# Moving residual additions, lambda's arithmetic, two weight splits and one product group in a two-layer decoder trunk on one NeuronCore

## The reference

```
proj = rmsnorm(x, g_mix[1]) @ w_in_b          # 768 differential queries, 256 memory queries
q    = rope(proj[..., :768])
lam  = exp(sum(lq1*lk1)) - exp(sum(lq2*lk2)) + lambda_init
p    = softmax(causal(q k^T / 8))             # 12 heads of 64, in pairs
a    = p[:, :, 0] - lam * p[:, :, 1]          # 6 pairs
o    = rmsnorm(a v, g_subln) * (1 - lambda_init)
m    = memory attention, 4 heads
x    = x + concat(o, m) @ w_out[1]
x    = x + top-2-of-8 expert SwiGLU(rmsnorm(x)), expert width 3584
out  = rmsnorm(x, g_final)
```

## Time and profile before

| | |
|---|---|
| median of 3 runs | 1523.36 us (1522.26 to 1524.27) |
| the profiled execution | 1524.27 us, span 1522.5 us |
| PE busy | 1460.5 us (96%) |
| DVE busy | 1147.5 us (75%) |
| ACT busy | 961.2 us (63%) |
| chain that ended last | PE 90%, DVE 5%, ACT 3% of the span |
| experts | from 542 to 1514 us of the span |

### The profile page before, as it was taken

The page is one execution under the profiler, slowest core; times in us unless marked ns, Lnnn a source line. Parts: engine busy times, 40 slices in busy tenths (PEclk is TensorE's granted clock), DMA queues, the critical chain, the costliest instruction groups (busy, mean ns, idle before and its releaser), DMA issues.

```text
span 1522.5 us, 19748 instructions
## 1 busy us (share of the span) xinstructions
PE 1460.5 (96%) x7414; PEld 1231.5 (81%) x7414; DVE 1147.5 (75%) x944; ACT 961.2 (63%) x883; POOL 24.4 (2%) x40
## 2 busy tenths in 40 slices
PE   7998899999898899999999999999999999999996
PEld 7975699999687678888888888888888888888885
DVE  4554444454667489889879879989988988987985
ACT  5652334434476387687777778677768678767773
POOL 1000020000000010000000000000000000000000
PEclk9995899999899899999999999999999999999999
DMA  9750275555532289999989999998998998998991
GB/s 298 256 186 28 84 273 170 170 194 181 175 112 83 98 315 388 396 326 394 396 321 373 395 376 343 393 379 328 396 390 310 393 396 323 387 396 322 391 396 40
DMA packets 204356, 440.42 MB, mean 289 GB/s; under 512 B 9232, under 2 KB 43184, under 8 KB 204304
## 3 DMA queue, kind: packets, MB, share of 16 engines
q1 hardware_dynamic: 201008, 428.37, 77.0%
q0 software_dynamic: 3296, 11.33, 2.1%
HBM read 430.76 MB, written 8.91 MB: 289 GB/s over the span
## 4 chain that ended last, share of the span: by engine, by line
PE 90%; DVE 5%; ACT 3%; issue 1%; DMA 0%; DVEq 0%; SPq 0%; ACTq 0%
PE ps L1422 28%; PE ps L1424 27%; PE ps L1423 27%; PE ps L1914 2%; DVE w_lo L881 1%; PE ps L1567 1%; ACT w_hi L496 1%; DVE H L912 1%; PE ps L1540 1%; PE ps L1448 1%; PE ps L1620 0%; PE ps L1884 0%; DMA raw<-in_w_mem_kv_dram 0%; ACT H L521 0%; PE ps L1885 0%
## 5 line engine op out<-in xcount | busy, mean ns | idle before, releaser
L1344 DVE TENSOR_TENSOR e_wlo<-raw,e_whi 128x2048 fp32r<-128x2048 f32 x336 | 751.1, 2285 | 89.7 <-ACT e_whi L815 89.7
L815 ACT ACTIVATE e_whi<-raw 128x2048 fp32r<-128x2048 f32 x336 | 621.0, 1915 | 39.7 <-PE ps L1424 37.0
L1422 PE MATMUL ps<-e_whi,act_hi 128*128 128x512 f32 x1344 | 529.0, 394 | 2.0 <-DVE act_lo L1300 1.5
L1424 PE MATMUL ps<-e_wlo,act_hi 128*128 128x512 f32 x1344 | 523.8, 390 | 0.0
L1423 PE MATMUL ps<-e_whi,act_lo 128*128 128x512 f32 x1344 | 523.2, 389 | 0.0
L1422 PEld LDWEIGHTS ps<-e_whi,act_hi 128*128 128x128 f32 x1344 | 252.4, 188 | 54.5 <-issue 3.0
L1424 PEld LDWEIGHTS ps<-e_wlo,act_hi 128*128 128x128 f32 x1344 | 252.3, 188 | 53.4
L1423 PEld LDWEIGHTS ps<-e_whi,act_lo 128*128 128x128 f32 x1344 | 252.5, 188 | 50.7
L881 DVE TENSOR_TENSOR w_lo<-raw,w_hi 128x2048 fp32r<-128x2048 f32 (+2 forms) x68 | 148.5, 2198 | 141.7 <-ACT w_hi L496 141.3
L496 ACT ACTIVATE w_hi<-raw 128x2048 fp32r<-128x2048 f32 (+2 forms) x68 | 124.1, 1839 | 66.8 <-PE ps L1424 59.1
L820 ACT ACTIVATE act_hi<-ps 128x512 fp32r<-128x512 f32 x56 | 33.6, 599 | 183.1 <-PE ps L1914 183.0
(11 more groups left out here) (243 smaller groups left out, 1091.9 us busy)
## 6 DMA issues: line engine op xcount, KB each, us to landing
raw<-in_w_exp_gate_dram SPq DMA_DIRECT2D x112, 1024.0 KB, 7.9
raw<-in_w_exp_up_dram SPq DMA_DIRECT2D x112, 1024.0 KB, 8.6
raw<-in_w_exp_down_dram SPq DMA_DIRECT2D x112, 1024.0 KB, 9.4
raw<-in_w_dense_gate_dram SPq DMA_DIRECT2D x11, 1024.0 KB, 5.4
raw<-in_w_dense_up_dram SPq DMA_DIRECT2D x11, 1024.0 KB, 5.4
raw<-in_w_dense_down_dram SPq DMA_DIRECT2D x11, 1024.0 KB, 5.8
raw<-in_w_out_dram SPq DMA_DIRECT2D x8, 1024.0 KB, 5.0
raw<-in_w_in_a_dram SPq DMA_DIRECT2D x7, 1024.0 KB, 9.7
```

The source lines that it names most:

```text
L815: nc.scalar.activation(e_whi[:, (s - NPRE) % E_SPLIT, :], raw[:, s % RAW, :], ACT.Copy)\
L1344: nc.vector.tensor_tensor(e_wlo[:, r, :], raw[:, s % RAW, :], e_whi[:, r, :].bitcast(F32), ALU.subtract).then_inc(lo_ready, 1)
L1422: nc.tensor.matmul(dst, l_hi, r_hi, start=start, stop=False)
L1424: return nc.tensor.matmul(dst, l_hi, r_lo, start=False, stop=stop)
```

## The change

It does five things. (1) The residual additions of both tiles stand before the normalisation of either, in all places where they were interleaved (`sums` is gone from `norm`). (2) VectorE's three lambda instructions, with their wait for `lam_a`, stand right behind the rotation of the second query tile. (3) VectorE writes slot o+2's remainder at i = D0 + 4 in place of D0 + 6. (4) Slot o+3 is split by ScalarE and VectorE inside the loop at i = D0 + 9, and TensorE does `memory_out(1)` inside the loop at i = D0 + 8, before that. (5) `heads_turn(1)` stands behind the two `out_product(2, ...)` in place of before them.

```
 ACT        if i == D0 + 4:
                split_to(o + 3)
+           if i == D0 + 9:
+               split_to(o + 4)
 ...
            head_rms(1)
-           split_to(o + 4)
            heads_high(1)

 DVE        def norm(signal, streams, new=True):       # sums=None is gone
                n = norms[0]
+               dve.wait_ge(gain_in, 16 * (n + 1))
                for t in range(TT):
-                   if sums is not None:
-                       sums(t)
-                   if t == 0:
-                       dve.wait_ge(gain_in, 16 * (n + 1))
 ...
+           dve.wait_ge(tile0_done, 2)
+           for half in range(2):
+               residual(0, half, 4 + half)
+           dve.wait_ge(slot_used, b)
+           for half in range(2):
+               residual(1, half, 6 + half)
+           norm(h_ready, 3)
-           norm(h_ready, 3, sums=dense_sums)
 ...
            rope(q_raw, 1, 20)
+           dve.wait_ge(lam_a, 1)
+           link(nc.vector.tensor_tensor(lamc[:, 4:5], lamc[:, 3:4], lamc[:, 2:3], ALU.subtract))
+           link(nc.vector.tensor_scalar(lamc[:, 5:6], lamc[:, 4:5], -LAMBDA_INIT, None, ALU.add))
+           link(nc.vector.tensor_scalar(gsub[:, :], gsub[:, :], 1.0 - LAMBDA_INIT, None, ALU.mult))
            split_to(k + 4)
            rope(k_raw, 2, 21)
            unit_max(NU0)
 ...        (the same four lines taken out behind unit_max(D0 + 1))
                if i == D0 + 4:
                    dve.wait_ge(mem_hi, 1)
                    nc.vector.tensor_tensor(act_lo[:, 6:8, :], ...).then_inc(mem_lo, 1)
-               if i == D0 + 6:
                    split_to(o + 3)
+               if i == D0 + 9:
+                   split_to(o + 4)
 ...
            head_norm(1)
-           split_to(o + 4)
            heads_low(1)

 PE             if i == D0 + 6:
                    pe.wait_ge(mem_lo, 1)
                    w_mem = take()
                    memory_out(0, w_mem)
+               if i == D0 + 8:
+                   memory_out(1, w_mem)
            heads_turn(0)
-           memory_out(1, w_mem)
            w0, w1 = take(), take()
            pe.wait_ge(heads_lo, 1)
            ...                                     # out_product(0), (1)
-           heads_turn(1)
            for t in range(TT):
                out_product(2, t, w1, 0)
+           heads_turn(1)
```

More of the change, by code:

```diff
@@ L899, in _, with norm @@
             norms = [0]
-            def norm(signal, streams, new=True, sums=None):
+            def norm(signal, streams, new=True):
                 n = norms[0]
+                dve.wait_ge(gain_in, 16 * (n + 1))
                 for t in range(TT):
[L905 to L908, removed]
                     if new:
@@ L919, in residual, with out_residual @@
                 nc.vector.tensor_tensor(xs, xs, ps[:, bank, :], ALU.add).then_inc(add_done, 1)
+            def out_residual(n, end):
+                dve.wait_ge(slot_used, end - 2)
+                for t in range(TT):
+                    residual(t, 0, 4 + t)
+                split_to(min(end + 2, NPRE))
+                dve.wait_ge(tile0_done, 2 * n + 1)
+                residual(0, 1, 6)
+                dve.wait_ge(slot_used, end)
+                residual(1, 1, 7)
             def unit_max(u):
@@ L1086, in _ @@
             split_to(first["dense"] + 1)
[L1087 to L1100, removed]
+            out_residual(0, first["dense"])
+            norm(h_ready, 2)
             turn()
@@ L1236, in _ @@
             head_norm(1)
-            split_to(o + 4)
             heads_low(1)
             split_to(NPRE)
-            def out_b_sums(t):
-                if t == 0:
-                    dve.wait_ge(tile0_done, 3)
-                else:
-                    dve.wait_ge(slot_used, o + 4)
-                for half in range(2):
-                    residual(t, half, ACC_BANK[t, half])
-            norm(h_ready, 4, sums=out_b_sums)
+            dve.wait_ge(tile0_done, 3)
+            for half in range(2):
+                residual(0, half, ACC_BANK[0, half])
+            dve.wait_ge(slot_used, o + 4)
+            for half in range(2):
+                residual(1, half, ACC_BANK[1, half])
+            norm(h_ready, 4)
             turn()
```

8 lines of the change are left out of this document (2 added, 6 removed).

## The result

The changed kernel takes **1537.22 us**, the median of four runs (1535.72 to 1537.95), beside 1523.82 (four runs, 1522.26 to 1524.3) for the kernel before: a ratio of 1.0091, 95% interval 1.0079 to 1.0103, or 13.9 us more. (The ratio is estimated over all runs of both kernels and is not the quotient of the two medians, which lie 13.4 apart.) The profiled execution took 1539.68 with a span of 1537.8, so from profile to profile the span grew by 15.3, where the sum of the terms was 15.1.

The account below looks back on a forecast made before the run. TensorE was taken as full in the experts and from 434 to 472 us, with engines waiting in turn from 472 to 494. Terms summed to +15.1 us on a median of 1523.36, giving 1538.5, range 1532.5 to 1544.0.

Parts of the forecast that it names:

- the clock holds: Rival: TensorE's clock stays up in all new gaps; +11.2 us in all, 1534.6; chance 0.20.
- A: After the first output projection: tile 1's addition fits ahead of tile 0's normalisation, next product earlier; -2.1 us.
- B: After the dense part: both additions fit before tile 0's root, transposes' copies come earlier; -2.5 us.
- N: Before the router: tile 0's normalisation already fits beside tile 1's products, exchange only moves a wait; 0 us.
- L: Before memory attention: VectorE's early lambda wait delays a key-weight slot, a maximum and unit 4's transposes; +5.5 us.
- C: Loop: slot o+2's early remainder waits for ScalarE, delaying unit 12's transposes 3.4, plus slow clock; +4.6 us.
- D: Loop: the second memory half's 12 products are hidden by nothing; +2.7 us.
- E: Loop: slot o+3's remainder waits for ScalarE and holds up the maximum of unit 18; +4.3 us.
- T: Tail: TensorE waits for both heads' remainders with nothing hiding them, partly at slow clock; +2.6 us.
- the second memory half runs at half clock too: Rival: the clock falls in each gap and through these loop products as well; +21.7 us, 1545; chance 0.10.
- Spare time: Rival: idle time in and before the loop absorbs the moved work; -6.1 us, 1517.3; chance 0.03.
- The parts don't overlap: Denies a rival: parts overlap, leaving one loop remainder's cost and half of lambda's; about +6 us, 1529.5; chance 0.07.

Follow-up runs that it names:

- The filled wait: Kernel before with slot o+2's remainder moved early and 16 unused 512-column products ahead of the waiting transposes: 1523.15 us, ratio 1.0019.
- The filled kernel: Kernel before with additions first, 6 memory products moved into the loop, and 18 or 19 unused transposes at each of three waits: 1508.92 us, ratio 0.9911.

## Why the prediction was right

The forecast was 1538.5, and 1537.22 came; of the rivals the nearest is 2.6 away (the clock holds, 1534.6). From the memory remainder to the heads' transposes the loop is 13.1 longer, where 9 to 14 were said. Step by step, each term as a difference of two steps' starts in the two traces:

| term | predicted | found | range stated |
|---|---|---|---|
| A additions, first output projection | -2.1 | -2.2 | -2.3 to -0.8 |
| B additions, dense | -2.5 | -2.3 | -2.7 to -1.2 |
| N additions, router | 0 | -0.2 | -0.3 to +1.3 |
| L lambda | +5.5 | +5.4 | 3.9 to 6.5 |
| C slot o+2's remainder | +4.6 | +6.3 | 3.4 to 5.9 |
| D memory half | +2.7 | +2.8 | 2.0 to 5.2 |
| E slot o+3 | +4.3 | +4.1 | 3.9 to 5.0 |
| T tail | +2.6 | +2.9 | 0.7 to 3.1 |

**A and B** came out as the in-order reasoning has it, and the additions alone show them again (-2.2 and -2.7). **D, E** are repeated by the two kernels that have them alone (+2.45, and 4.4 on top). **T**: two gaps of 2.11, "near 2 us twice"; the wait for the remainder took 3.65 from the heads' transposes (3.62 was said), the 36 products 10.41 (10.1), the last transposes' way 2.93 (2.9).

**L came out by another path than the one worked.** Its idle times are what was said (9.10 for "some 9", 3.52 for "near 4"), and the maximum is 5.8 late. But the prediction has the transposes wait for that maximum's chain ("follow the reciprocal", 5.1 late), and they don't. Before, the reciprocal was over at 442.36 and TensorE, busy without a break, reached the transposes only at 443.21; now it is over at 441.13 and they start at 441.60, again with no idle time ahead. What makes them late is TensorE itself: its slot's first product comes 3.87 later behind the scores of unit 4, and the 12 products at the lower clock add 1.49. That the two ways give 5.1 and 5.4 is chance; with the clock held, the chain would have been the later of the two, by some 1.2 (an estimate: 441.60 less 1.49, beside 441.13 and 0.15 to the start).

**C was mis-sized**, and lies outside its own bounds. Its idle part is what was said (the transposes +3.34 later relative to the memory remainder, "+3.4"). The clock part was taken as a half-way value of 1.2 and given at most 2.5; it measured 2.95: the 12 products behind the gap took 5.13 instead of 2.82 (+2.31), and the values ahead of them were slow as well (+0.64). In the two other kernels with the same unfilled wait it measured 2.73 and 1.80, so the size varies by a microsecond between executions, and 2.5 is not its bound. The filled wait shows that this part is the clock: with the clock held, the stretch behind the wait is as short as before (18.81 and 18.87), without it 2.5 longer.

**Two things were not foreseen.** In the tail the clock fell a second time, behind the second 2.11 (0.57 from 524 to 528), which put +1.8 between the product behind the transposes and the last one; the experiment with only these transposes moved shows it too (+3.78 against the +2.3 of the waits). And other slow stretches moved in the other direction: -1.2 ahead of every edit, -0.5 in the dense part, -0.8 between the query products and the scores of unit 4, -0.8 in the router. All in all -1.2 - 2.2 - 0.5 - 2.3 - 0.8 + 5.4 + 6.3 + 2.8 + 4.1 + 2.9 + 1.8 - 0.2 - 0.8 is the +15.1 of the first expert product, but for 0.2 of rounding. The sum hit the span because C's excess and the tail's second fall (+3.5) were met by these (-3.3); that is luck, and the range was there for it.

**The rivals.** That the clock holds in all gaps (+11.2) is refuted: it fell in or behind those of 3.52 and 4.23 and behind the second 2.11. Not every fall needs such a gap, though: near the end of the loop the kernel before has one as well, and term E hardly has a clock part (from unit 17's transposes to the heads' 6.72, before 6.39). That the second memory half runs at half clock too is refuted by D = 2.8 and 2.45; the first half did, in C. (That rival's sum takes 4.0 for the additions where the others take 4.6, without a reason; with 4.6 it is 1544.5.) Spare time is not usable: the maximum of unit 13, at 473.36 before, is at 475.78 though the trace is 1.6 ahead there, and the memory half's move gave the tail nothing back. The parts don't overlap by anything measurable (22.2 one by one, 21.3 together, in their stretch of the traces).

**What stays open.** The additions alone gained 7.6 where the waits in the trace give 4.9, and lambda alone lost 7.8 where its stretch gives 5.1. The filled kernel shows the clock to be worth 4.5 at three such waits, and the same instructions behind the same wait differ by 1.5 in the dense part of two kernels (187.14 and 188.65); how much of each of these two differences in the times that makes, no run here separates. Nor does a run show why the clock falls at 491 in the kernel before, or why it comes back sooner in some executions than in others.

## What to carry to other kernels

An instruction that waits holds all that stands behind it on its engine (lambda's made a slot's remainder start 6.7 us later against the scores of unit 4, and TensorE's product of it 3.9): before moving one forward, look up in the trace when what it waits for is over, and let it stand behind everything that is ready sooner. The same exchange that won 2.2 us where the moved work was ready (an addition ahead of a normalisation that had to wait) lost 3 to 5 where it was not. Work that stands behind a transpose or a copy whose result comes back through two engines is cover; moving it away turns it into idle time. And a gap of 3.5 to 4.2 us of TensorE cost its length and a slow stretch of 1.5 to 3 us behind it here, except at the loop's end, where the clock falls without it too; products with unused results prevented it where the gap itself stayed.

## What the runs showed of the hardware

With sixteen unneeded products of 512 columns a kernel was 5.8 us faster by its median, 2.5 of it shown to be theirs, and 55 unneeded transposes of 128x128 gave another one 4.5. Transposes alone, 2.24 us of them and 0.83 of idle time in the place of a wait of 2.9, held the clock at 1.00. Behind the same wait of 4.2 us the slow stretch cost 1.80, 2.73 and 2.95 in three kernels, and the clock also fell where no idle piece was longer than 1.11. The way from the router's first product to the experts, the same code in all, took from 16.10 to 18.57. The same code reached its first output projection's end 1.2 us apart in two executions, and had a granted clock of 0.89 and of 0.77 over the same 15 us in two others, so differences below some 2 us in this kernel were read from steps within a trace and not from the times.
